# The low parts of a two-layer encoder's FFN, divided anew between VectorE and GpSimd, and three orders around them

## The reference

```python
D_MODEL = 1024
D_FF = 2816
def rmsnorm(x, g):
    xf = x.astype(jnp.float32)
    y = xf * lax.rsqrt(jnp.mean(xf * xf, axis=-1, keepdims=True) + EPS)
    return (y * g.astype(jnp.float32)).astype(x.dtype)

def swiglu(x, w_gu, w_dn):
    g, u = jnp.split(x @ w_gu, 2, axis=-1)
    return (jax.nn.silu(g) * u) @ w_dn
...
    # layer 0: h = h + mlstm(...);  layer 1: h = h + sliding-window attention(...)
        h = h + swiglu(rmsnorm(h, norm_ffn[l]), w_gate_up[l], w_down[l])
```

## Time and profile before

| | |
|---|---|
| median of three runs | 2462.68 us |
| the profiled execution | 2462.17 us, span 2460.4 us |
| TensorE busy | 98% |
| VectorE busy | 67% |
| ScalarE busy | 35% |
| GpSimd busy | 40% |
| granted TensorE clock, mean | 0.996 |

### The profile page before, as it was taken

One profiled execution on the slowest core, in us unless ns is written; L12 is line 12 of the kernel. 1 busy time (PEld: TensorE's weight loads), 2 busy tenths in 40 slices (PEclk: granted clock), 3 DMA queues, 4 the chain that ended last, 5 costly groups with the idle time before them and its releaser, 6 DMA issues. The chain is left out here.

```text
span 2460.4 us, 42910 instructions
## 1 busy us (share of the span) xinstructions
PE 2412.8 (98%) x16730; PEld 2338.6 (95%) x16730; DVE 1654.7 (67%) x2544; ACT 867.0 (35%) x1765; POOL 992.0 (40%) x814
## 2 busy tenths in 40 slices
PE   9999999999999999999999999999999999999998
PEld 8989999999999999999999989889999999999997
DVE  6445454439767667688879656757867766778776
ACT  5223232326222222243425556436322222243334
POOL 1222222422544444444447343335544444444542
PEclk9999999999999999999999999999999999999999
DMA  4445565211223223264422133210132232354423
GB/s 160 144 131 147 166 178 188 63 36 37 86 89 102 84 92 102 83 207 156 151 86 60 46 81 103 58 34 28 64 109 82 93 100 86 104 189 146 142 82 123
DMA packets 303533, 259.50 MB, mean 105 GB/s; under 512 B 52856, under 2 KB 261164, under 8 KB 303300
## 3 DMA queue, kind: packets, MB, share of 16 engines
q1 hardware_dynamic: 303140, 256.70, 33.9%
q10 hardware_dynamic: 192, 0.04, 0.0%
HBM read 180.95 MB, written 77.54 MB: 105 GB/s over the span
## 5 line engine op out<-in xcount | busy, mean ns | idle before, releaser
L429 POOL TENSOR_TENSOR wh<-raw,wh 128x512 fp32r<-128x512 f32 x360 | 542.7, 1508 | 669.4 <-ACT wh L423 669.3
L423 ACT ACTIVATE wh<-raw 128x512 fp32r<-128x512 f32 x360 | 227.4, 632 | 716.4 <-PE psum L732 341.4
L732 PE MATMUL psum<-xh,wh 128*128 128x292 f32 (+1 forms) x2560 | 458.4, 295 | 0.3 <-POOL wh L429 0.2
L732 PEld LDWEIGHTS psum<-xh,wh 128*128 128x128 f32 x2560 | 381.7, 188 | 0.8 <-POOL wh L429 0.8
L2765 PE MATMUL psum<-xh,wh 128*128 128x384 f32 (+1 forms) x792 | 274.6, 347 | 1.4 <-DVE fr_tmp L2955 0.5
L732 PE MATMUL psum<-xl,wh 128*128 128x292 f32 (+1 forms) x1280 | 275.3, 297 | 0.0
L2765 PE MATMUL psum<-xl,wh 128*128 128x384 f32 (+1 forms) x792 | 270.0, 341 | 0.0
L2765 PE MATMUL psum<-xh,wl 128*128 128x384 f32 (+1 forms) x792 | 268.8, 339 | 0.0
L955 DVE TENSOR_TENSOR h<-h,psum 128x584 f32<-128x584 f32 (+1 forms) x280 | 204.9, 752 | 80.9 <-PE psum L752 80.7
L752 PE MATMUL psum<-ffn_slot,wh 128*128 128x292 f32 (+1 forms) x1536 | 209.5, 297 | 7.8 <-DVE h L955 5.1
L752 PEld LDWEIGHTS psum<-ffn_slot,wh 128*128 128x128 f32 x1536 | 206.8, 189 | 8.8 <-issue 8.8
(11 more groups left out here) (329 smaller groups left out, 5064.4 us busy)
## 6 DMA issues: line engine op xcount, KB each, us to landing
raw<-in_w_gate_up SPq DMA_DIRECT2D x160, 256.0 KB, 3.0
raw<-in_w_down SPq DMA_DIRECT2D x80, 256.0 KB, 3.1
ffn_form_d<-ffn_gate_quarters SPq DMA_DIRECT2D x50, 292.0 KB, 2.1
ffn_form_d<-ffn_gate_quarters SPq DMA_DIRECT2D x50, 288.0 KB, 2.1
raw<-in_a_w_in SPq DMA_DIRECT2D x24, 512.0 KB, 4.9
ffn_slot_raw<-ffn_form_d SPq DMA_DIRECT2D x16, 584.0 KB, 4.7
fr_qkv<-qkv_d SPq DMA_DIRECT2D x36, 256.0 KB, 3.8
ffn_slot_raw<-ffn_form_d SPq DMA_DIRECT2D x16, 576.0 KB, 4.9
```

The costliest lines, as they stand in the source:

```text
L423: act.activation(self.ring(p)[0], self.quarter(b), ACT.Copy).then_inc(self.w_hi, 1)
L429: pool.tensor_tensor(lo, self.quarter(WEIGHT_OF[p % 7]), hi.bitcast(F32), ALU.subtract).then_inc(self.w_lo, 1)
L732: y = pe.matmul(psum[:, bank + c, 0:N], w[:, k, :], x[:, N * c:N * c + N], start=(FRESH[i] and k == 0 and m == 0), stop=(k == 3 and m == 2 ...
```

## The change

It has two parts, both within the FFN.

1. Three low parts in seven move to GpSimd. Of the seven forms of each chunk, GpSimd makes the low parts of forms 1, 3 and 5 (new `hidden_low`), and VectorE those of 0, 2, 4 and 6. GpSimd also makes the four low parts of t1 at entry (new `t1_low`). They are counted by `t4_lo`.
2. Three orders change. At entry, the first SiLU part comes ahead of the t2 high parts on ScalarE, which take the order 2, 3, 0, 1; VectorE makes the products and t4 sums earlier, the t2 low parts among them, and the last two t3 sums only behind the first copy out of PSUM. At a pair's end, one form sum instead of three is made in the odd group, and two go behind the first copy of the next group; the form sum that was fourth stays; one of them (a12 - a11) is now put in another buffer. The last weight sum of a group is made one product later.

```diff
         self.weight_lo(pool, 3)
+        for k in range(4):
+            self.t1_low(pool, k)
         for g in range(WIDE_GROUPS + DOWN_GROUPS):
             p = 7 * g
             self.product_lo(pool, p)
+            if g == WIDE_GROUPS:
+                self.hidden_low(pool, 0, 3, self.t4_lo)
+            last_chunk = (g - 19) // 2
...
             self.product_lo(pool, p + 1)
+            if g > WIDE_GROUPS and g % 2 and last_chunk < CHUNKS:
+                self.hidden_low(pool, last_chunk, 3, self.t4_lo)
...
             self.product_lo(pool, p + 3)
+            if g == WIDE_GROUPS:
+                self.hidden_low(pool, 0, 5, self.t4_lo)
+            if g > WIDE_GROUPS and g % 2 and last_chunk < CHUNKS:
+                self.hidden_low(pool, last_chunk, 5, self.t4_lo)
...
             self.product_lo(pool, p + 5)
+            if g == WIDE_GROUPS - 1:
+                self.hidden_low(pool, 0, 1, self.t4_lo)
             self.product_lo(pool, p + 6)
+            if g >= WIDE_GROUPS and g % 2 == 0 and (g - 18) // 2 < CHUNKS:
+                self.hidden_low(pool, (g - 18) // 2, 1, self.t4_lo)
...
+    def t1_low(self, pool, k):
+
+        hi, lo = self.wide_x(3, k)
+        pool.wait_ge(self.t_raw, self.z["t_raw"] + 4 + k + 1)
+        pool.wait_ge(self.x_hi, self.z["x_hi"] + 24 + k + 1)
+        pool.tensor_tensor(lo, self.wide_raw(3, k), hi.bitcast(F32), ALU.subtract).then_inc(self.t4_lo, 1)
+
+    def hidden_low(self, eng, kk, j, done):
+
+        m = 7 * kk + j
+        hi, lo = self.combo(m)
+        eng.wait_ge(self.hid_hi, self.z["hid_hi"] + m + 1)
+        eng.tensor_tensor(lo, self.hidden_raw(m), hi.bitcast(F32), ALU.subtract).then_inc(done, 1)
...
             t1_hi(k)
-        for k in range(4):
+        gate_part(0)
+        for k in (2, 3, 0, 1):
             t2_hi(k)
-        gate_part(0)
         gate_part(1)
...
-                if not up and pair > 1 and i == 0:
-                    dve.wait_ge(self.hid_sum, self.z["hid_sum"] + 4 * (pair - 2) + 3)
+                if not up and pair > 1 and i in (0, 3):
+                    dve.wait_ge(self.hid_sum, self.z["hid_sum"] + 4 * (pair - 2) + (3 if i else 1))
...
         def weight_sums(g, i):
-            if g and i == 0:
+            if g and i == 1:
                 self.weight_sum(dve, g, 3)
...
-                if g % 2 and g < 19 and i in (5, 6):
-                    for n in ((0,), (1, 2))[i - 5]:
+                if g % 2 and g < 19 and i == 6:
+                    form_sum(pair, 0)
+                if g and g % 2 == 0 and i in (0, 2):
+                    for n in ((1, 2), (), (3,))[i]:
                         form_sum(pair, n)
-                if g and g % 2 == 0 and i == 2:
-                    form_sum(pair, 3)
-                if g == 19 and i >= 4:
-                    for j in ((0,), (1,), (2, 3))[i - 4]:
-                        hidden_lo(0, j)
+                if g == 19 and i in (4, 6):
+                    hidden_lo(0, i // 2 - 2 if i == 4 else 2)
...
                 for kk, j in hidden_steps(g, i):
-                    hidden_lo(kk, j)
+                    if j % 2 == 0:
+                        hidden_lo(kk, j)
```

More of the change, by code:

```diff
@@ L348, in store_sum @@
         sp.wait_ge(self.hid_sum, self.z["hid_sum"] + 4 * (pair - 1) + n + 1)
-        src, form, x = ((self.part[:, 1], 4, 4), (self.quad[:, 1], 3, 1), (self.part[:, 0], 2, 4), (self.quad[:, 3], 6, 3))[n]
+        src, form, x = ((self.part[:, 1], 3, 4), (self.part[:, 0], 2, 4), (self.quad[:, 1], 4, 1), (self.quad[:, 3], 6, 3))[n]
         sp.dma_start(self.form_d[pair - 1, form], src[:, 0:self.H]).then_inc(self.hid_st[x], 16)
@@ L741, in down_product @@
             if sub == 0:
-                pe.wait_ge(self.hid_lo, self.z["hid_lo"] + 7 * kk + i + 1)
+                if i % 2:
+                    pe.wait_ge(self.t4_lo, self.z["t4_lo"] + 6 + 3 * kk + (i + 1) // 2)
+                else:
+                    pe.wait_ge(self.hid_lo, self.z["hid_lo"] + 4 * kk + i // 2 + 1)
             hi, lo = (w.rearrange("p (k n) -> p k n", k=2) for w in self.ring(p))
@@ L959, in form_sum @@
             a11, a12, a22, a21 = (self.quad[:, q, 0:H] for q in range(4))
-            f2, f4 = self.part[:, 0, 0:H], self.part[:, 1, 0:H]
+            f2, f3 = self.part[:, 0, 0:H], self.part[:, 1, 0:H]
             base = self.z["hid_sum"] + 4 * (pair - 1)
@@ L1030, in vector @@
                 recip(c + 1)
-        for k in range(4):
-            t_low(3, k, 24 + k + 1)
         for c in range(3):
             product(0, c, 3 * c + 2)
+        for k in (2, 3):
+            t4_raw(k)
+        t_low(2, 2, 29)
+        t_low(2, 3, 30)
         take(self.up, 1, 0, 3, 10)
         product(1, 0, 10)
-        for k in (2, 3):
+        for k in (0, 1):
             t4_raw(k)
+        t_low(2, 0, 31)
         take(self.up, 1, 1, 4, 11)
         product(1, 1, 11)
-        for k in (0, 1):
-            t4_raw(k)
+        t_low(2, 1, 32)
         for k in range(2):
             t3_raw(k)
-        t_low(2, 0, 29)
         take(self.up, 1, 2, 5, 12)
         product(1, 2, 12)
-        for k in range(1, 4):
-            t_low(2, k, 28 + k + 1)
         def weight_sums(g, i):
-            if g and i == 0:
+            if g and i == 1:
                 self.weight_sum(dve, g, 3)
@@ L1054, in weight_sums @@
                 self.weight_sum(dve, g + 1, i - 4)
-        for k in (2, 3):
-            t3_raw(k)
         for g in range(WIDE_GROUPS):
@@ L1060, in vector @@
                 wide_out(g, i)
+                if g == 0 and i == 0:
+                    for k in (2, 3):
+                        t3_raw(k)
                 weight_sums(g, i)
```

40 lines of the change are left out of this document (19 added, 21 removed).

## The result

The changed kernel takes 2478.23 us (median of 5 runs, 2476.59 to 2481.58), the kernel before beside it 2462.23 (5 runs): a ratio of 1.0069, with a 95% interval of 1.0057 to 1.0080. It is slower by 16 us, outside the range given, and on the side of the rival "Slower, by the lock". The profiled execution took 2476.59 us with a span of 2474.8, that is 14.4 more than before in the span.

The account below looks back on a forecast made before the run. TensorE, at work in 98% of the span, was taken as the bound, only its gaps winnable. Entries 0 and -1.5, pair ends -8.0, first down products +9.0, other down groups +2.0 gave +1.5 us: 2464 us, range 2452 to 2474.

Parts of the forecast that it names:

- Slower, by the lock: Rival, down groups and first entry: each long GpSimd low part holds VectorE for its whole length; +12.6, 2475 us; 17%.
- the pot: TensorE's winnable gaps: entry 12.2, pair ends 8.2, first down products 8.6 us, one more clock loss; together about 30 us.
- The lock: VectorE and GpSimd: one waits until the other's instruction ends; PSUM reads untouched; moved low part 2.8 us on GpSimd.
- Entry: Group 0 of each FFN: 0 in the first (-3.4 to +3.6), -1.5 us in the second (-3 to 0).
- Pair ends: Waits behind the copy out of PSUM: fewer form sums ahead make it earlier; -8.0 of 8.2 us, ends -8.2 and 0.
- First down products: Around groups 19 and 20: GpSimd late on form 1, 5.4 us stall, lower clock; +4.5 per FFN, +9 in all.
- The other down groups: Twelve more GpSimd low parts per FFN make VectorE's sum 0.4 to 0.9 us late per chunk; +2, ends 0 and +7.
- there is room on the average: Other down groups: GpSimd busy 28.5 and VectorE 47.8 of 60 us, so the moved low parts fit on average.
- the wait before (19,6) with the clock down behind it: Sign for the forecast: 4 to 6 us gap before product 6 of group 19, released by GpSimd's weight low part.
- a new gap of over 1 us: Sign against the forecast: new gaps of over 1 us in every down group.

Follow-up runs that it names:

- e10: Changed kernel, form low parts back on VectorE, chunk 0's form 3 later, down-group weight sum at old place, t1 low parts on VectorE in both FFNs: 2453.12 us.
- e13: As e10, but the four t1 low parts on VectorE in the first FFN only, on GpSimd in the second: 2454.22 us.
- e1: Changed kernel with all form low parts back on VectorE; its orders and the t1 low parts on GpSimd stay: 2456.3 us.
- e7: e1 with the weight sum A12 - A11 back behind product 0 in the down groups: 2453.93 us.
- e4: Changed kernel with each of GpSimd's form low parts made by two instructions of 576 elements: 2477.24 us.
- e8: Changed kernel with GpSimd's form 3 of chunks 1 to 4 ahead of the weight low part of product 1 of the odd group: 2478.53 us.
- e11: As e10 but t1 low parts on GpSimd, and form 3 alone of chunks 1 to 4 on GpSimd: 2467.09 us, against 2451.89 without.
- e12: As e10 but t1 low parts on GpSimd, and form 5 alone of chunks 1 to 4 on GpSimd: 2470.84 us, against 2451.89 without.
- e14: e12 with GpSimd's form 5 three products later, behind the weight low part of product 6 of the odd group: 2454.39 us.
- e5: Changed kernel with VectorE's weight sum A12 - A11 back behind product 0 in the down groups: 2503.39 us.
- e6: e1 with VectorE's form 3 low part of chunk 0 later, behind the sum into h of product 0 of group 20: 2453.6 us.

## Why the prediction was wrong, point by point

*What bounds the kernel, and the pot.* Right: TensorE's gaps were the place to look, and three of the five stretches moved as worked out.

*The lock.* Right as a mechanism, and every meeting looked at fits it: VectorE's 1152-element low part takes 1.35 us alone, 2.59 beside a GpSimd instruction of 576 elements, 3.83 beside one of 1152. GpSimd's takes 2.6 to 2.7 us alone; I had 2.8.

*Entry.* Right in time: 0 and -1.5 forecast, +0.6 and -2.6 in the trace. TensorE waited where it was forecast in the first FFN, at (0,1), 605 to 608, and at (0,4), 618 to 622:

```profile
607.71 0.83 PE L763 MATMUL psum<-xh,wh 128*128 128x292 f32 x2 [3.97 <-DVE ffn_up L896]
...
620.79 0.54 PE L763 MATMUL psum<-xh,wh 128*128 128x292 f32 x2 [1.00 <-POOL wh L429]
```

In part that is two errors that met. By the traces of e10 and e13 the orders alone win 1.8 us there (5.2 for 7.0), and t1 on GpSimd loses 2.5. The four low parts ended at 593.6 and not at 594.9 (4 x 1.44 from 587.3 is 593.1), and the wait at (0,1) was followed by a lower clock that the term did not have.

*Pair ends.* Right: -8.2 for -8.0.

*First down products.* Right in total, +8.2 for +9.0, with the stall of 5.6 us where 5.4 was forecast, and the clock down for longer than I took (6.8 us in each FFN by the profile's records, where the first FFN alone had 3.4 before). The 5.6 is partly luck: GpSimd could start only 1.2 us after TensorE fell idle, and not 0.15 before, since the loads of forms 0 and 1 landed late for ScalarE (why, no run tests), and then needed 4.4 us and not 5.5, since it met VectorE only once. And e1 shows that the orders without any moved form have 11.1 us of gaps there, so that the moved forms cost 7.6 of the 18.7.

*The other down groups: the step that failed.* "I take +2, ends 0 and +7": it was 17.6. The +2 is even less than the 3.2 that its own 0.4 us in 8 chunks make. Three faults, in the order of their size. First, the argument "there is room on the average", from 28.5 and 47.8 us of 60 in the earlier trace rows. The lock makes the two engines one resource, and the low parts are not spread: seven products in fourteen carry them all. From e7, VectorE's and GpSimd's rows there:

```profile
2253.34 0.68 DVE L450 TENSOR_TENSOR raw<-raw 128x512 f32<-128x512 f32 x1
2253.94 1.35 DVE L478 TENSOR_TENSOR ffn_slot<-ffn_slot_raw,ffn_slot 128x1152 fp32r<-128x1152 f32 x1
2255.21 1.41 DVE L973 TENSOR_TENSOR h<-h,psum 128x576 f32<-128x576 f32 x2
2256.54 0.68 DVE L454 TENSOR_TENSOR raw<-raw 128x512 f32<-128x512 f32 x1
```

```profile
2255.27 1.29 POOL L429 TENSOR_TENSOR wh<-raw,wh 128x512 fp32r<-128x512 f32 x1 [1.85 <-ACT wh L423]
```

By start to start the weight sum has 0.60 us, the form low part 1.27, the PSUM sums 1.33: 3.20 in a product of 3.18. GpSimd's 1.29 lie exactly beside the PSUM sums, the only part of VectorE's work that it does not hinder. A form low part of 2.6 us does not fit into 1.33, and at none of the places tried in these seven products did it go without a wait (e4, e8, e11, e12); at the one place tried in the other seven it did (e14). The durations for this stood in the earlier trace rows, the order in the kernel's own lists. Second, I priced the lateness at 0.4 to 0.9 us once per chunk; it is 1.4 in three chunks of each FFN (8.4 in all) and 4 to 5 us in chunk 1's groups 20 and 21. The form sums of the last pair stand there too, which may be why; no run takes them away. Third, the later weight sum had no price in the text; it happened to spare the change 25 us (e5). Without that luck it would have been slower by 1.7%.

*The rivals.* "Slower, by the lock", 2475 us, had the right mechanism, place and sign, at 17%; it had 0.8 us in each of 8 chunks where it was 2.2 on the average (17.6 / 8). That its total came within 3 us is partly luck: it had +3.6 for the first entry, where +0.6 was measured, and 10.6 for the first down products, where it was 8.2. Of the signs that were named, the wait before (19,6) with the clock down behind it came as written, and so did, in every odd down group, the one that was to speak against the forecast: a new gap of over 1 us.

## What to carry to other kernels

Where two engines block each other as these do, moving work from the quicker to the slower one makes the shared resource busier: 1.27 us became 2.6. Count the time under the lock for both engines together, product by product in the most crowded stretch and not on the average, and look for the windows that are not under it (here the PSUM reads). Price every moved line of a diff, also one 0.7 us instruction that only changes its neighbour: which of two long instructions starts first decided 25 us here.

## What the runs showed of the hardware that was not expected

The same wait is sometimes followed by a lower clock and sometimes not. Before (0,4) of the second FFN TensorE stood 1.99 us in e1 and 1.95 us in e6, which differ up to there in the place of one low part, some 660 us earlier. The windows behind it (columns of the earlier trace rows; e1, then e6):

```profile
1748.00:1752.00 4.00, 4.00 (x21) 4.00 (x20) 2.48 (x2) 1.21 (x2) 3.82 (x3) 0.57 0.14 39
```

```profile
1747.00:1751.00 4.00, 4.00 (x32) 4.00 (x32) 3.77 (x4) 1.84 (x3) 4.00 (x4) 1.00 0.13 36
```

The one has the lower level for most of the time and starts 21 matmuls, the other 32. In all thirteen traces with the changed kernel's order at this entry (0,4) starts 2.2 us late, and in eight of them the lower level follows. That is 1.6 us in a product, so gaps of single profiled runs of this kernel compare only to within one or two such losses. And a GpSimd instruction can make VectorE busier than it was: 37 us more in the page's busy time, with 38 instructions fewer.
